# Two changes of order: ScalarE's work per slot of a latent attention, and VectorE's work per slot of a windowed attention

## What is computed

```python
# first block
q, k, v, u, gate_a, gate_b = split(rms_norm(x) @ w_in)   # q: 16 heads of 128
y_a = windowed_gqa(rms_norm(q), rms_norm(k), v, sink) @ w_attn_o
...                                  # state space part, gates, expert retrieval
# second block: dilated attention, layer norm, then the latent attention
h = x @ w_in                         # widths 512, 512, 64, 2048
c_q, c_kv, k_pe, z = split(h)
q = rms_norm_2(c_q, q_norm) @ w_uq           # per head 128 + 64 (rotary)
kv = rms_norm_2(c_kv, kv_norm) @ w_ukv       # per head k 128 + v 128
o = causal_mla_attention(q_nope, q_pe, k_nope, k_pe, v)
y = (o * silu(z)) @ w_out
```

## Time and profile before

| what | value |
|---|---|
| time of the kernel, median of 3 runs | 3758.59 us (3754.63 to 3760.09) |
| the profiled execution's own time | 3760.41 us |
| its span in the profile | 3758.6 us |
| TensorE busy | 3312.7 us (88%) |
| GpSimd busy | 2160.5 us (57%) |
| VectorE busy | 1657.4 us (44%) |
| ScalarE busy | 1335.7 us (36%) |
| mean granted TensorE clock | 0.972 of full speed |

### The profile page before, as it was taken

The page is one execution under the profiler, slowest core; times in us unless marked ns, Lnnn a source line. Parts: engine busy times, 40 slices in busy tenths (PEclk is TensorE's granted clock), DMA queues, the critical chain, the costliest instruction groups (busy, mean ns, idle before and its releaser), DMA issues.

```text
span 3758.6 us, 38271 instructions
## 1 busy us (share of the span) xinstructions
PE 3312.7 (88%) x13402; PEld 2343.8 (62%) x13402; DVE 1657.4 (44%) x2525; ACT 1335.7 (36%) x2016; POOL 2160.5 (57%) x1144
## 2 busy tenths in 40 slices
PE   7999989997688778777777779999999999989997
PEld 6788878885243234332322348888888888867775
DVE  6888245316657447544744542222123223321332
ACT  4666466444111001000100014444444444444553
POOL 1000366887544545455555528788778877865555
PEclk9999999998899999999999999999999999988998
DMA  6444444566999999999999965455545555543334
GB/s 190 132 124 123 152 137 142 191 215 245 414 418 420 422 420 420 421 421 422 421 418 422 421 274 175 168 180 172 171 172 175 174 170 167 173 159 125 129 132 140
DMA packets 239642, 936.34 MB, mean 249 GB/s; under 512 B 37728, under 2 KB 40032, under 8 KB 172896
## 3 DMA queue, kind: packets, MB, share of 16 engines
q0 software_dynamic: 73728, 536.90, 34.4%
q1 hardware_dynamic: 157664, 392.22, 31.6%
q10 hardware_dynamic: 8064, 4.80, 0.4%
HBM read 927.02 MB, written 2.10 MB: 247 GB/s over the span
## 4 chain that ended last, share of the span: by engine, by line
PE 53%; DMA 24%; POOL 9%; issue 5%; DVE 4%; ACT 3%; ACTq 1%; DVEq 0%; POOLq 0%; SPq 0%
PE products L671 31%; DMA arena<-peer_up_in,arena 21%; PE products L1339 8%; POOL weights_low L614 8%; PE products L1868 6%; DMA arena<-peer_down_in,arena 4%; POOL arena L1813 1%; DVE arena L1822 1%; PE products L1090 1%; PE products L2401 1%; PE products L2376 1%; PE products L1196 1%; ACTq L2316 1%; PE products L1113 1%; PE products L1375 0%
## 5 line engine op out<-in xcount | busy, mean ns | idle before, releaser
L614 POOL TENSOR_TENSOR weights_low<-arena,weights_high 128x1024 fp32r<-128x1024 f32 x496 | 1215.0, 2457 | 437.5 <-ACT weights_high L602 436.0
L1868 PE MATMUL products<-arena 128*128 128x512 f32 x1984 | 935.8, 616 | 318.9 <-DMA arena<-peer_up_in,arena 236.8
L602 ACT ACTIVATE weights_high<-arena 128x1024 fp32r<-128x1024 f32 x612 | 645.9, 1058 | 1058.1 <-PE products L671 1023.4
L671 PE MATMUL products<-weights_high,input_high 128*128 128x512 f32 x2432 | 996.0, 410 | 16.4 <-DVE weights_low L614 9.6
L671 PE MATMUL products<-weights_low,input_high 128*128 128x512 f32 x2432 | 956.7, 393 | 0.0
L671 PE MATMUL products<-weights_high,input_low 128*128 128x512 f32 x2432 | 953.8, 392 | 0.0
L1868 PEld LDWEIGHTS products<-arena 128*128 128x128 f32 x1984 | 367.3, 194 | 870.8 <-issue 444.4
L1822 DVE SCALAR_TENSOR_TENSOR arena<-arena 128x2048 f32<-128x2048 f32 x256 | 586.0, 2292 | 522.4 <-DMA arena<-peer_down_in,arena 522.0
L1813 POOL DMA_INDIRECT arena<-peer_up_in,arena x256 | 383.4, 1498 | 524.2 <-PE products L1868 504.1
L671 PEld LDWEIGHTS products<-weights_high,input_high 128*128 128x128 f32 x2432 | 461.2, 190 | 114.3 <-issue 14.5
L671 PEld LDWEIGHTS products<-weights_low,input_high 128*128 128x128 f32 x2432 | 459.9, 189 | 100.8
(11 more groups left out here) (321 smaller groups left out, 2957.3 us busy)
## 6 DMA issues: line engine op xcount, KB each, us to landing
arena<-dsa_in SPq DMA_DIRECT2D x320, 512.0 KB, 3.4
arena<-w_in_in SPq DMA_DIRECT2D x128, 512.0 KB, 3.8
arena<-mla_wide_in SPq DMA_DIRECT2D x97, 512.0 KB, 3.4
arena<-w_attn_o_in SPq DMA_DIRECT2D x32, 512.0 KB, 4.4
arena<-w_out_in SPq DMA_DIRECT2D x32, 512.0 KB, 4.6
arena<-peer_w_query_in SPq DMA_DIRECT2D x32, 512.0 KB, 4.5
arena<-dsa_w_out_in SPq DMA_DIRECT2D x32, 512.0 KB, 3.7
arena<-glu_w_b_in SPq DMA_DIRECT2D x16, 512.0 KB, 3.7
```

Source lines behind the costliest of these rows:

```text
L602: nc.scalar.activation(w_hi[:, u % RING, :, at], ring[:, u % RING, :, at], ACT.Copy).then_inc(hi_made, 1)
L614: ops.tensor_tensor(w_lo[:, u % RING, :, at], ring[:, u % RING, :, at], w_hi[:, u % RING, :, at].bitcast(F32), op=ALU.subtract).then_inc(l ...
L671: mm = nc.tensor.matmul(PS[:, bank(b) + t, 0:width], x[:, x0 + n, at], y, start=n == 0 and m == 0, stop=n == len(parts) * PK - 1 and m == 2)
L1868: mm = nc.tensor.matmul(PS[:, SUM_BANKS[q]], diag[:, d % ROWS], row[:, q * NC:(q + 1) * NC], start=h % 2 == 0 and n == 0, stop=bool(last))
```

## The change

In `a_dve` the block that scales the query rows moves behind the block that divides a head's probabilities. In the latent attention ScalarE's slot function is cut in two: `mla_leave` holds what empties the accumulator banks and the rounding of a finished pair's result, and is called ahead of `mla_hi(act, n + RING)`; `mla_act` keeps the heads' work and the transposed blocks, behind it. No instruction is added or removed, and no wait is.

```diff
--- before.py
+++ after.py
@@ -976,12 +976,6 @@
             if a == 0:
                 scale_heads(dve, B_K, 0, 0, ks_rows)
             i, m = divmod(a - 2 * PARTS, PARTS)
-            if 0 <= i < QUADS and m == 0:
-                if i == 0:
-                    dve.wait_ge(ys_in, 16 * 8 * SSM_KT)
-                if i >= 2:
-                    dve.wait_ge(turn_ready, after(X_Q + 2 * (i - 2) + 1))
-                scale_heads(dve, B_Q + i, 1, i, rows[:, i % 2])
             for h, k in a_heads(a):
                 if k == 1:
                     dve.wait_ge(exp_done, after(H_A + h))
@@ -992,6 +986,12 @@
                     for t in range(NT):
                         n = nc.vector.tensor_scalar(PA[:, h % 2, t], PA[:, h % 2, t], exp_inv[:, h % 2, t:t + 1], None, ALU.mult)
                     n.then_inc(p_ready, 1)
+            if 0 <= i < QUADS and m == 0:
+                if i == 0:
+                    dve.wait_ge(ys_in, 16 * 8 * SSM_KT)
+                if i >= 2:
+                    dve.wait_ge(turn_ready, after(X_Q + 2 * (i - 2) + 1))
+                scale_heads(dve, B_Q + i, 1, i, rows[:, i % 2])
             for h, k in a_heads(a):
                 if k == 0:
                     dve.wait_ge(score_made, after(S_A + h))
@@ -1511,7 +1511,7 @@
                 mla_head_pe(pe, h, k)
             mla_turn_pe(pe, n)
 
-        def mla_act(act, n):
+        def mla_leave(act, n):
 
             kind, i, u = M_ORDER[n - 1] if n else (None, 0, 0)
             if (kind, u) in (("cq", PARTS - 1), ("ckv", PARTS - 1)):
@@ -1531,13 +1531,16 @@
             if (kind, u) == ("z", PARTS - 1):
                 mla_made(act, kind, i, u)
                 nc.scalar.activation(rows2[:, 0], mla_bank(kind, i), ACT.Silu).then_inc(evac[1], 2)
-            for h, k in mla_heads(n):
-                mla_head_act(act, h, k)
-            mla_turn_act(act, n)
             for p in range(MLA_PAIRS):
                 if n == M_START[p + 1] + 10:
                     act.wait_ge(o_read, 1 + H_M + 2 * p + 2)
                     nc.scalar.activation(YHR[:, 2 * p:2 * p + 2], ZM[:, 2 * p:2 * p + 2], ACT.Copy).then_inc(lhs_hi, 1)
+
+        def mla_act(act, n):
+
+            for h, k in mla_heads(n):
+                mla_head_act(act, h, k)
+            mla_turn_act(act, n)
 
         def mla_dve(dve, n):
 
@@ -2737,6 +2740,7 @@
             turn_hi(act, X_MLA_IN)
 
             for n in range(len(M_ORDER)):
+                mla_leave(act, n)
                 if n + RING < len(M_ORDER):
                     mla_hi(act, n + RING)
                 mla_act(act, n)
```

## The result

The changed kernel takes 3728.02 us (median of 4 runs, 3727.59 to 3733.66); the kernel before took 3758.62 us beside it (3754.63 to 3760.09). The ratio is 0.9918, with a 95% interval of 0.9906 to 0.9931: faster, by 30.6 us between the medians, or 0.8%. The prediction was 3731 us.

What follows compares the result with a forecast made beforehand. TensorE was taken as the bound (53% of what ended last), so edits gain only its idle time. Terms summed to 29.1 us, taking the profiled 3760.4 to 3731.3, stated as 3731; range 3722 to 3744.

Steps and rivals of the forecast that it cites:

- VectorE in slot 24: First attention: dividing before scaling query rows cuts TensorE's 6.98 us wait to some 1.4 and regains clock; 8.6 us.
- ScalarE between "uq" and "ukv": Latent attention: copying banks out before rounding weights removes five TensorE waits for line 1529; 8.8 us with overlap.
- norm of "ckv": Latent attention, behind the narrow "kpe" part: root and scaling finish earlier, removing TensorE's 4.59 us wait; 4.8 us.
- silu of the first "z": Latent attention: silu starts about two microseconds earlier, removing TensorE's 1.47 us wait; 1.6 us with overlap.
- wait for line 1393: Latent attention: an earlier bank copy takes some 0.6 of TensorE's 0.7 us wait for a turned block; 0.7 us.
- the last pair: Latent attention's end: result rounded one part earlier, VectorE still held by GpSimd, TensorE's wait 4.18 to 1.45; 4.6 us.
- I leave that slow part as it is: First part behind "kpe": its 5.1 us at 1.2 GHz assumed unchanged; 2.3 us more if at full clock.
- 1.9: Part behind the last pair's result: clock stays high, so 4.65 us becomes 2.7; 1.9 us regained.
- held operations: Rival, latent attention: moved roundings shift GpSimd onto VectorE work, delaying divisions; at most 14 us, 3738 to 3745; chance 0.23.
- The stall stays: Rival, first attention: division moves but roots or next waits keep the stall; only latent attention gains, 3740; chance 0.05.
- the moved copy does nothing: Rival, latent attention: ScalarE waits for VectorE's share before the copy, making its weights equally late; 3745; chance 0.03.
- slower: Rival, latent attention: weight rounding delayed 7.8 us, beyond the 4.6 us cover, so TensorE runs dry; 3771; chance 0.03.

Runs made afterwards that it cites:

- the repeat: The changed kernel measured once more with no further edit, as reference for later runs: 3729.48 us, ratio 0.9922 against the kernel before.
- the first edit alone: The kernel before with only VectorE's scaling of query rows moved behind the division in the first attention: 3752.03 us, ratio 0.9975.
- the copies alone: The kernel before with only the q and k copies out of the accumulator (line 1529) ahead of the rounding of part n+4: 3750.51 us, ratio 0.9974.
- the weights rounded last: The changed kernel with part n+4's weight rounding behind all ScalarE's other work of slot n in the latent attention: 3730.27 us, ratio 0.9921 against the kernel before.
- the squares and roots alone: The kernel before with only the two latent-attention norms' squares and roots ahead of the rounding of part n+4: 3753.46 us, ratio 0.9982.

## Why the prediction was right

The time (3728.0 against 3731) and the sum (28.7 us of edits against 29.1) both came out, and no single term carried it. Part of the closeness is luck: the medians differ by 30.6 us (31.9 for the repeat), 2 us more than the stretches add up to, which lies inside the scatter of the unedited stages, and the first two terms missed to opposite sides. Term by term:

| term | predicted | measured |
|---|---|---|
| VectorE in slot 24 | 8.6 | 8.40 |
| ScalarE between "uq" and "ukv" | 8.8 | 9.49 |
| norm of "ckv" | 4.8 | 4.08 |
| silu of the first "z" | 1.6 | 1.64 |
| wait for line 1393 | 0.7 | 0.48 |
| the last pair | 4.6 | 4.25 |
| a wait for line 1483 | not counted | 0.38 |

- **VectorE in slot 24.** "What is late next" was line 804, with a stall of 1.4 us; it is 1.37. The clock of the window is 1.00, and both the stall and the slow products are gone. The run with this edit alone gives 8.36, so it needs nothing of the other. The mechanism is shown; that the size came to 8.4 and not 7.1 depends on how long the clock stayed low in the execution of before.
- **Between "uq" and "ukv".** All five waits vanished. The term was too small because I gave a stall 0.16 us beyond its idle time. In four of the pairs, the two distances between parts around the wait shrank by 1.99 us together for a wait of 1.69, so it costs 0.3 beyond it.
- **Norm of "ckv".** The wait vanished. "I leave that slow part as it is" is the mis-sized step: the slow products behind it became more, not the same (below). Expected 4.8, measured 4.08 here and 4.1 to 4.2 in five other runs, but 5.06, 5.54 and 5.39 in three more.
- **The last pair.** VectorE is held again, as the row had it, for 2.44 us, and TensorE waits 1.49 (1.45 forecast). "1.9" for the part behind it is mis-sized: I set a time from the part's first product to ScalarE's next rounding (4.65) against a spacing of parts (2.7), and the first takes longer also at the full clock (3.15). Like against like, from first product to first product, it fell from 4.45 to 2.89: 1.56 us. The 1.7 in slot 24 has the same flaw; there 1.5 came back, 8.40 less the 6.9 up to line 880.
- **Silu and line 1393.** As forecast, within 0.25 us. A third small wait, 0.2 us for line 1483 in a head, went too; I had not listed it, and it was worth 0.38.

Of the rivals, the *held operations* do occur. Line 1483 and the pair's low half by form, latent attention, first before and then after (busy time, mean ns, idle time before them):

```profile
L1483 DVE TENSOR_SCALAR arena<-arena 128x128 f32<-128x128 f32 x16 | 12.4, 777 | 1.2
L1570 DVE TENSOR_TENSOR arena_rounded<-arena,arena_rounded 128x512 fp32r<-128x512 f32 x8 | 9.4, 1179 | 35.9 <-ACT arena_rounded L1540 35.9
```

```profile
L1483 DVE TENSOR_SCALAR arena<-arena 128x128 f32<-128x128 f32 x16 | 17.0, 1060 | 1.2
L1573 DVE TENSOR_TENSOR arena_rounded<-arena,arena_rounded 128x512 fp32r<-128x512 f32 x8 | 12.8, 1598 | 7.1 <-ACT arena_rounded L1537 7.1
```

The two lines together take 8.0 us more of VectorE's time (17.0 + 12.8 against 12.4 + 9.4). In both traces an instruction of this form of line 1483 takes 0.29 us where GpSimd stands still at its start, and those of 0.86 us and more all overlap one of GpSimd's. None of the held time is waited for, apart from the last pair's: no wait for line 1483 is left. The rival had the mechanism right and the price wrong, since in the rest of a pair VectorE is ahead of TensorE. *The stall stays* fell with the first edit alone, *the moved copy does nothing* with the copies alone, and *slower* with the weights rounded last. For the last of these the runs show that the cover exceeds the moved work; its size was not measured.

## What to carry to other kernels

When one engine is the bound, list its waits in the edited stage and put each together from three numbers: the idle time, the products that run at the slow clock behind it, and the next input that is late. Where an engine rounds weights ahead into a ring and also empties an accumulator, let the accumulator go first: the ring has slack and the accumulator has a reader. An operation that is held by another engine is no loss until its result is the last one awaited, so move its start by one slot before adding a semaphore.

## What the runs showed of the hardware

**The clock behind narrow products.** In the "kpe" part TensorE works through products of 64 columns without a wait; nonetheless the granted clock falls to 1.2 GHz 4.5 to 5.4 us into it (thirteen executions), and stays there into the wide products that follow. In the changed kernel no stall stands in front of these, and yet they begin slow:

```profile
3381.39 0.77 PE L1339 MATMUL products<-weights_high,input_high 128*128 128x512 f32 x1
...
3386.66 0.63 PE L1339 MATMUL products<-weights_high,input_high 128*128 128x512 f32 x1
...
3387.37 0.39 PE L1339 MATMUL products<-weights_low,input_high 128*128 128x512 f32 x1
```

At 1.2 GHz a product is listed with 0.63 us, at 2.4 GHz with 0.39. Read so from the first narrow product on:

| kernel | narrow until the clock falls | slow wide products | first narrow product to the turned block in "z" |
|---|---|---|---|
| before | 4.6 us | 4.0 us | 28.46 us |
| after | 4.7 us | 5.7 us | 24.31 us |
| the squares and roots alone | 5.4 us | 3.6 us | 22.69 us |
| the changed kernel again | 5.2 us | 3.1 us | 22.67 us |

With the stall gone, the slow stretch in the changed kernel became 1.7 us longer. At half the speed that costs 0.85 us, and 4.59 + 0.3 less 0.85 is about the 4.08 that was measured. In the two lower rows the clock fell later and came back earlier. The last row is the very kernel of the second, so the point at which the clock changes is not set by the instructions alone. The Trainium skill, TensorE: Matmul & The Clock Gate, Part 1, says that the activity is watched in windows that run free and do not start with the kernel; the spread agrees, though no run here shows the windows themselves.

**Which stalls bring the clock down.** The waits of 7.0 and 4.2 us did (windows at 0.66 and 0.81 in the kernel before), in each of the five and four executions that have them. Those of 1.37 and 1.49 us did not (windows at 1.00), in any. Between them lies a wait of 2.26 us for line 804, ahead of both edits and in every trace. Behind it the clock was low in some executions and not in others. 424 to 428 us, first in the changed kernel and then in that with the copies alone:

```profile
424.00:428.00 4.00, 3.42 (x11) 2.90 (x12) 0.53 (x1) 1.33 (x2) 4.00 (x2) 0.57 0.12 25
424.00:428.00 4.00, 3.79 (x21) 3.22 (x22) 0.16 (x1) 1.21 (x3) 4.00 (x2) 1.00 0.13 28
```

The wait ends within 0.4 us of the same time in both, and all code up to there is the same. At this length the wait alone does not decide.

**Offsets between executions.** The same code reaches the first attention up to 9 us earlier or later. About half of this is the clock in one place. From TensorE's wait near 406 us to its wait for line 804 it takes 18.8 us in six of the thirteen profiled executions and 23.6 in the other seven. In the six, the clock is 1.00 between 407 and 419 us, in the seven 0.57 to 0.70. The kernel before and the changed kernel:

```profile
407.00:419.00 12.00, 12.00 (x57) 11.15 (x58) 2.03 (x2) 0.00 (x0) 0.00 (x0) 0.59 0.27 89
407.00:419.00 12.00, 12.00 (x75) 10.65 (x74) 2.55 (x3) 4.40 (x9) 0.54 (x1) 1.00 0.39 111
```

The edits do not sort the two groups: the changed kernel is in the first, its repeat in the second. What decides between them is not shown. The offset is not kept either: the repeat begins the first attention's stretch 4.5 us later than the first execution of the changed kernel, and its last latent product comes 0.8 us earlier. Whole executions follow the clock in the same way. Of nine with the squares and roots alone the fastest took 3745.39 us at a mean clock of 0.975 and the slowest 3763.15 at 0.969. Two single profiles of this kernel can therefore differ by more than the last pair's whole term, with no cause in the edit.
